# Final normalisation of a one-layer decoder: the weight vector multiplied in before the root is known, the row scale split between VectorE and ScalarE

## The chip, the cores and the metric

One core of one Trainium2 chip runs the whole program. The metric is the device time of one execution in microseconds (us). Differences of under 0.5% are taken as no difference that a measurement of this kernel can tell.

## The reference

One inference step of a hybrid decoder layer for 1024 prompt tokens and 32 sample tokens, D = 1024. The first two thirds (projection, RWKV-7 mixing, windowed attention, output projection, routing) are not touched. What matters here is the end:

```python
x = x + hier_moe(rmsnorm(x, norm_ffn_g))      # 16 experts, 2 per token, SwiGLU
y = rmsnorm(x, norm_final_g)                  # x * rsqrt(mean(x*x) + 1e-6) * norm_final_g
```

Every token needs, for its output row, the sum of squares of the finished row, the root of it, and a product with a scale per row and with the weight vector `norm_final_g` (`gfin`, spread over all 128 partitions).

## The kernel before

The experts are worked off one after the other, e = 0 to 15 (`NE` = 16), in an order sorted at run time. For each expert TensorE does four quarters f = 0 to 3 of gate and up (`gate_up`, L1544, 32 matmuls of 128x128 each), and then `down` (L1567, two halves of eight 128x512 matmuls). In TensorE's program order `down` of expert e - 1 stands after the first quarter of expert e, so the end of the program reads: quarter 0 of expert 15, down of 14, quarters 1, 2, 3 of expert 15, down of 15. For each quarter ScalarE takes the silu (L2087) and VectorE multiplies with the up half (`product`, L2792). Two banks of PSUM alternate between the quarters: quarter f of an expert is not started before the product of quarter f - 2 has read its bank, and down of an expert waits for all four products of it.

For experts 0 to 12 the weighted outputs are scattered into `x_dram`, the residual rows in HBM. The last three (13, 14, 15, `LAST` = 3) are dealt with apart: their rows are gathered out of `x_dram` into `xsA[0]` to `xsA[2]`, `sums` (L2891) adds the outputs of the expert on VectorE, and the sums are normalised by themselves and scattered straight to the outputs by GpSimd (`put`, L3052, two for each of the three experts).

All rows of `x_dram` are loaded when the scatters of expert 12 have landed: nine tiles `final_rows(t)`, t = 0 to 8, tiles 0 to 7 in the region `XF` (which held expert weights before), tile 8 (32 sample tokens) in a slot of `X2`. Those rows that the last three experts still touch are normalised and stored too, and are overwritten afterwards by `put`.

The final normalisation lies in the time of the last two experts:

- **Expert 14, ScalarE** (`before_last`): a square with a sum over the row for `xsA[0]` (f = 0) and for tiles 0 to 8 (f = 1 to 3, three each, L2103); after the last, one root over the ten sums (L2106, with a load of the table of the square root), and a dummy silu that loads the silu table again (L2110).
- **Expert 15, VectorE**: after product 0 it takes the reciprocal of the ten roots (L2948), `own` writes the normalised rows of expert 13 (L2899), `sums(1, 0)` and `sums(1, 1)` for expert 14, and `bulk(t)` for the nine tiles, each one instruction that does row scale and weight vector at once (L2896). Six `bulk` stand before product 1, three between product 1 and product 2.
- **Expert 15, ScalarE** (`at_last`): f = 0: a square of `xsA[1]`, which waits for `sums(1, 1)`; f = 2: its root, and the silu table again; f = 3: the table of the root. The silu of quarter f stands ahead of step f.
- **SP** stores the tiles in the order 0 to 8 (L742), each when its `bulk` is done (semaphore `fin`); the stores count on `h2o0` and `h2o1`.
- **GpSimd** waits for all nine stores, then for `fn_dve` of each group, and issues the six `put`.
- **The end**: `sums(2, h)` for the two halves of down of expert 15, squares, root, reciprocal and a last scaling by row (L2971) into `XF[:, 0, :]`, then the last two `put`. VectorE and ScalarE wait for the stores (`h2o0`, `h2o1`) before that, since `XF[:, 0, :]` is also tile 0.

Of the kernel before, what the change touches and what calls it, by code (L numbers as in the profile page):

```python
# [30 lines left out]
NE = NG * EPG  # L31
# [109 lines left out]
def program(nc, i, o):  # L141

    ctx = ExitStack()
    with ctx:
# [261 lines left out]
        YST = [stored(ACC, k) for k in range(2)]  # L406
        NDOWN = downs(NE)
        NOUT = NE + NTAIL
        FA, FD = 16, 4
        H2O = [32 * 4 + 16, 32 * 5 + 16]  # L410

        ps = ctx.enter_context(nc.psum_tensor("ps", [P, 8, 512], F32))
# [99 lines left out]
        def _(sp):  # L512
# [199 lines left out]
            def one_round(r, later):  # L712
                if later:
                    sp.wait_ge(s["ya_ps"], NDOWN * r)
                    alone(sp)
                    sp.wait_ge(s["fn_dve"], FD * r)
                    alone(sp)
                    for e in range(2):
                        x = expert(e)
                        load_pair(x, GU[e])  # L720
                        load_part(x, e, 2)
                    load_pair(expert(2), GU[2])
                for e in range(NE - 2):
                    sp.wait_ge(s["gu_ps"], 4 * (NE * r + e + 1))
                    alone(sp)
                    if GU[e] in GU[e + 1:]:
                        load_pair(expert(e + 1 + GU[e + 1:].index(GU[e])), GU[e])
                    else:
                        for k in range(2):
                            sp.wait_ge(s[f"yst{k}"], YST[k] * (r + 1))  # L730
                            alone(sp)
                        for n, (a, b) in enumerate(XL):
                            sp.dma_start(XF[:, a:b, :], x_rows[:, a:b]).then_inc(s[f"x{n}"], 16)
                        sp.dma_start(final_rows(NT), x_dram[SEQ:TOK]).then_inc(s["x3"], 16)
                    sp.wait_ge(s["ya_ps"], NDOWN * r + downs(e + 1))
                    alone(sp)
                    load_part(expert(e + 2), e % 2, 2)

                for t in range(NTT):
                    sp.wait_ge(s["fin"], NTT * r + t + 1)  # L740
                    dst = y_rows[t * P:(t + 1) * P, :] if t < NT else ys_rows
                    sp.dma_start(dst, final_rows(t)).then_inc(s[f"h2o{t % 2}"], 16)  # L742
                sp.wait_ge(s["h2o0"], H2O[0] + 16 * 5 * (r + 1))
                alone(sp)
                sp.wait_ge(s["h2o1"], H2O[1] + 16 * 4 * (r + 1))
                alone(sp)
# [894 lines left out]
        def _(act):  # L1641
# [455 lines left out]
            def one_round(r, later):  # L2097
# [23 lines left out]
                def before_last(f):  # L2121
# [7 lines left out]
                    if f == 3:  # L2129
                        act.wait_ge(s["fn_act"], fa + 10)  # L2130
                        root(10, stat[:, 0:10]).then_inc(s["fn_act"], 1)
                        table(ACT.Silu, 52)

                def at_last(f):
                    if f == 0:
                        act.wait_ge(s["yo_dve"], out0 + ACC + 1 + tails_to(ACC + 1) + 1)
                        act.wait_ge(s["fn_dve"], FD * r + 1)
                        square(eyA[:, 0, :], xsA[1], 32).then_inc(s["fn_act"], 1)
                    elif f == 2:
                        act.wait_ge(s["fn_act"], fa + 12)  # L2140
                        root(33, stat[:, 32:33]).then_inc(s["fn_act"], 1)
                        table(ACT.Silu, 53)
                    elif f == 3:
                        table(ACT.Sqrt, 54)
# [14 lines left out]
                        elif e == NE - 1:  # L2159
                            at_last(f)  # L2160

                act.wait_ge(s["h2o0"], H2O[0] + 16 * 5 * (r + 1))
                act.wait_ge(s["yo_act"], g0 + NE)
                square(X2[:, 2, 0:512], xsA[2][:, 0:512], 42).then_inc(s["fn_act"], 1)
                act.wait_ge(s["yo_dve"], out0 + NOUT)
                square(X2[:, 2, 512:], xsA[2][:, 512:], 43).then_inc(s["fn_act"], 1)
                act.wait_ge(s["fn_act"], fa + 15)
                act.wait_ge(s["fn_dve"], FD * r + 3)
                root(45, stat[:, 43:44], 0).then_inc(s["fn_act"], 1)

# [9 lines left out]
        def _(dve):  # L2180
# [623 lines left out]
            def one_round(r, later):  # L2804
# [85 lines left out]
                    x = xsA[k][:, 512 * h:512 * (h + 1)]  # L2890
                    dve.scalar_tensor_tensor(x, ps[:, 5 + h, :], wA[:, e:e + 1], x, ALU.mult, ALU.add).then_inc(s["yo_dve" if h else "yo_act"], 1)  # L2891

                def bulk(t):
                    n = toks(t)
                    x = final_rows(t)
                    dve.scalar_tensor_tensor(x, x, stat[0:n, 20 + t:21 + t], gfin[0:n, :], ALU.mult, ALU.mult).then_inc(s["fin"], 1)  # L2896

                def own(dst, k, rstd):
                    dve.scalar_tensor_tensor(dst, xsA[k], stat[:, rstd:rstd + 1], gfin, ALU.mult, ALU.mult).then_inc(s["fn_dve"], 1)  # L2899

                def after_last(f):
                    if f < 2:
                        for t in range(3):
                            bulk(3 * f + 3 + t)
                    elif f == 2:
                        dve.wait_ge(s["fn_act"], fa + 13)
                        again(dve.reciprocal(stat[:, 34:35], stat[:, 33:34]))
                        own(eyA[:, 0, :], 1, 34)

                slot_marks()  # L2910
                if later:
# [21 lines left out]
                for e in range(1, NE - 1):  # L2933
                    product(g0 + e, e, 0)
                    if 1 < e <= ACC:
                        rows_out(r, e - 1)
                    elif e > ACC:
                        for h in range(2):
                            sums(e - 1 - ACC, h)
                    product(g0 + e, e, 1)  # L2940
                    turn(r, e + 1)
                    for f in range(2, 4):
                        product(g0 + e, e, f)

                product(g0 + NE - 1, NE - 1, 0)
                dve.wait_ge(s["shift_in"], 64)
                dve.wait_ge(s["fn_act"], fa + 11)
                again(dve.reciprocal(stat[:, 20:30], stat[:, 10:20]))  # L2948
                own(eyA[:, 1, :], 0, 29)
                sums(1, 0)  # L2950
                bulk(0)
                sums(1, 1)
                bulk(1)
                bulk(2)
                after_last(0)
                for f in range(1, 4):
                    product(g0 + NE - 1, NE - 1, f)
                    after_last(f)
                sums(2, 0)
                dve.wait_ge(s["fn_act"], fa + 14)  # L2960
                dve.tensor_scalar(stat[:, 44:45], stat[:, 42:43], 1.0 / D, RMS_EPS, ALU.mult, ALU.add).then_inc(s["fn_dve"], 1)
                dve.wait_ge(s["h2o0"], H2O[0] + 16 * 5 * (r + 1))
                dve.wait_ge(s["h2o1"], H2O[1] + 16 * 4 * (r + 1))
                dve.wait_ge(s["yo_act"], g0 + NE)
                dve.tensor_tensor(XF[:, 0, 0:512], xsA[2][:, 0:512], gfin[:, 0:512], ALU.mult)
                sums(2, 1)
                dve.wait_ge(s["yo_dve"], NOUT * (r + 1))
                again(dve.tensor_tensor(XF[:, 0, 512:], xsA[2][:, 512:], gfin[:, 512:], ALU.mult))
                dve.wait_ge(s["fn_act"], fa + 16)
                again(dve.reciprocal(stat[:, 46:47], stat[:, 45:46]))  # L2970
                dve.tensor_scalar(XF[:, 0, :], XF[:, 0, :], stat[:, 46:47], None, ALU.mult).then_inc(s["fn_dve"], 1)  # L2971
                assert steps[0] == STEPS

            one_round(0, False)
# [8 lines left out]
        def _(pool):  # L2983
# [136 lines left out]
            pool.wait_ge(s["h2o0"], H2O[0] + 16 * 5 + 16 * 5 * past)  # L3120
            alone(pool)
            pool.wait_ge(s["h2o1"], H2O[1] + 16 * 4 + 16 * 4 * past)
            for k, out in enumerate((eyA[:, 1, :], eyA[:, 0, :], XF[:, 0, :])):
                e = ACC + k
                alone(pool)
                pool.wait_ge(s["fn_dve"], FD * past + (1, 2, 4)[k])
# [28 lines left out]
```

## Time and profile before

| | us |
|---|---|
| three runs | 1167.63, 1170.05, 1172.68 (median 1170.05) |
| the profiled execution | 1167.85 |
| span of it, first to last instruction | 1166.0 |
| time around the span | 1.85 |

Times in the profile count from the start of the span. An engine name with q (SPq, POOLq) is the sequencer or DMA queue of that engine; PEld is TensorE's weight load. In a timeline row the first figure is the start, the second the duration, and the bracket holds the idle time of the engine just before it and what ended it.

### The profile page before, as it was taken

The numbers are of one execution on the slowest core, as the hardware profiler recorded it, in microseconds if no ns is written. First come the engines' busy times: TensorE is split into PE (matmuls) and PEld (weight loads), VectorE is DVE, ScalarE is ACT, GpSimd is POOL, SyncE is SP. The second block draws the span as 40 slices with busy tenths as digits, with TensorE's granted clock in tenths as the row PEclk, the third lists the DMA queues.
The fourth block names the chain that finished last, engine by engine and source line by source line (L and its number), as shares of the span: only waits on it lengthen the run. The fifth ranks groups of instructions, "written<-read, shape, count | busy, mean of one in ns | idle before, by whom it ended". The sixth has DMA issues, their size and how long they took to land.

```text
span 1166.0 us, 23360 instructions
## 1 busy us (share of the span) xinstructions
PE 1099.5 (94%) x10010; PEld 773.1 (66%) x10010; DVE 499.0 (43%) x993; ACT 358.8 (31%) x816; POOL 299.7 (26%) x197
## 2 busy tenths in 40 slices
PE   5999999999999988888899999899999999999994
PEld 4666666666666667767654444587877887888782
DVE  3300566538865586686734422453111211221144
ACT  3110545554434375755621311210000000000052
POOL 0000000001110169999900000015313232233102
PEclk9999999999999999999999999889999999999997
DMA  6611100001110220002051751239999899999874
GB/s 206 162 36 39 59 19 19 19 19 41 33 30 19 26 48 3 4 4 57 4 203 26 266 209 67 95 140 397 380 389 320 315 320 330 336 314 303 279 268 168
DMA packets 69523, 174.06 MB, mean 149 GB/s; under 512 B 20708, under 2 KB 41895, under 8 KB 65172
## 3 DMA queue, kind: packets, MB, share of 16 engines
q1 hardware_dynamic: 61492, 151.92, 36.6%
q0 software_dynamic: 7920, 20.57, 7.1%
q8 instruction: 81, 1.33, 0.5%
q14 instruction: 30, 0.25, 0.1%
HBM read 147.45 MB, written 27.75 MB: 150 GB/s over the span
## 4 chain that ended last, share of the span: by engine, by line
PE 86%; DVE 9%; issue 2%; ACT 1%; SPq 0%; DMA 0%; POOLq 0%; POOL 0%; DVEq 0%
PE ps L810 23%; PE ps L1544 21%; PE ps L1328 10%; PE ps L1567 9%; PE ps L1573 1%; PE ps L889 1%; PE ps L913 1%; PE ps L902 1%; PE ps L1080 1%; DVE arena L2383 1%; PE ps L1202 1%; PE ps L1039 1%; PE ps L1408 1%; PE ps L1216 1%; PE ps L1138 1%
## 5 line engine op out<-in xcount | busy, mean ns | idle before, releaser
L810 PE MATMUL ps<-arena 128*128 128x352 f32 (+1 forms) x960 | 296.4, 465 | 2.1 <-issue 1.9
L1544 PEld LDWEIGHTS ps<-arena 128*128 128x128 f32 x2048 | 247.8, 192 | 10.5 <-issue 6.6
L1544 PE MATMUL ps<-arena 128*128 128x128 f32 (+4 forms) x2048 | 250.8, 284 | 3.3 <-DVE arena L2792 2.4
L810 PEld LDWEIGHTS ps<-arena 128*128 128x128 f32 x960 | 179.6, 190 | 105.1 <-issue 9.5
L1328 PE MATMUL ps<-arena 128*128 128x512 f32 x256 | 116.4, 597 | 0.7 <-DVE arena L2468 0.7
L1567 PE MATMUL ps<-arena 128*128 128x512 f32 x256 | 112.7, 593 | 1.4 <-DVE arena L2792 1.4
L2087 ACT ACTIVATE arena<-ps 128x128 f32<-128x128 f32 (+4 forms) x64 | 18.3, 285 | 270.3 <-PE ps L1544 270.3
L2990 POOL TENSOR_TENSOR arena<-arena 128x1024 f32<-128x1024 f32 x4 | 11.4, 2858 | 320.2 <-DVE arena L2269 320.2
L2792 DVE TENSOR_TENSOR arena<-arena,ps 128x128 f32<-128x128 f32 (+4 forms) x64 | 19.1, 299 | 172.6 <-ACT arena L2087 172.6
L1567 PEld LDWEIGHTS ps<-arena 128*128 128x128 f32 x256 | 47.5, 190 | 55.4 <-issue 53.6
L1328 PEld LDWEIGHTS ps<-arena 128*128 128x128 f32 x256 | 46.8, 190 | 52.8 <-issue 51.0
L3055 POOL DMA_INDIRECT arena<-h_dram,idxG x60 | 57.9, 964 | 82.8 <-DVE arena L2773 44.9
L3048 POOL DMA_INDIRECT x_dram<-arena,rowA x13 | 21.1, 1622 | 140.8 <-DVE arena L2802 102.1
L1658 ACT COPY arena<-ps 128x353 f32<-128x353 f32 (+1 forms) x40 | 18.0, 451 | 113.2 <-PE ps L810 113.2
L2799 DVE TENSOR_SCALAR arena<-ps,arena 128x512 f32<-128x512 f32 x13 | 9.8, 751 | 77.9 <-PE ps L1567 77.9
L3009 POOL TENSOR_TENSOR arena<-arena 128x1024 f32<-128x1024 f32 (+4 forms) x40 | 41.0, 1026 | 2.8
L2773 DVE STREAM_TRANSPOSE arena<-arena 128x256 f32<-128x256 f32 x68 | 37.4, 607 | 2.5 <-DMA arena<-h_dram,idxG 2.5
L1875 ACT COPY arena<-ps 64x256 f32<-64x256 f32 x80 | 29.4, 367 | 24.4 <-DVE ps L2405 23.1
L2314 DVE SCALAR_TENSOR_TENSOR arena<-ps,arena 128x1024 f32<-128x1024 f32 (+1 forms) x16 | 18.5, 1158 | 41.7 <-PE ps L889 41.7
L2581 DVE TENSOR_TENSOR arena<-arena,ps 128x512 f32<-128x512 f32 x16 | 11.0, 687 | 58.5 <-PE ps L1328 58.2
L1069 PE MATMUL ps<-arena 64*64 64x64 f32 x1280 | 29.6, 226 | 6.7 <-DVE arena L2389 5.8
L1728 ACT ACTIVATE arena<-arena 128x256 f32<-128x256 f32 (+1 forms) x64 | 30.9, 486 | 12.5 <-DVE arena L2320 12.5
(440 smaller groups left out, 1524.3 us busy)
## 6 DMA issues: line engine op xcount, KB each, us to landing
arena<-in_w_exp_gate SPq DMA_DIRECT2D x16, 2048.0 KB, 10.0
arena<-in_w_exp_up SPq DMA_DIRECT2D x16, 2048.0 KB, 14.5
arena<-in_w_exp_down SPq DMA_DIRECT2D x16, 2048.0 KB, 14.0
arena<-in_w_in SPq DMA_DIRECT2D x16, 512.0 KB, 3.8
arena<-in_x_prompt SPq DMA_DIRECT2D x9, 512.0 KB, 4.4
x_dram<-arena SPq DMA_DIRECT2D x9, 512.0 KB, 3.6
h_dram<-arena SPq DMA_DIRECT2D x8, 512.0 KB, 2.6
out_y_prompt<-arena SPq DMA_DIRECT2D x8, 512.0 KB, 3.5
```

The costliest lines, as they stand in the source:

```text
L810: last = pe.matmul(ps[:, q % 2, 0:m], wr[:, n % 3, k, :], hT[:, k, a:a + m], start=(k == 0), stop=(k == KB - 1))
L1069: last = pe.matmul(ps[row(e ^ u), 4 * b + u, j * CH:(j + 1) * CH], L[row(e), b, u, e, j, 0:CH], TL[row(e), b, JB * u + j, :], start=True, ...
L1328: return pe.matmul(ps[0:n, 4 * (q % 2) + hf, :], MX[:, b, t * P:t * P + n], wo[b][:, hf * 512:(hf + 1) * 512], start=(b == 0), stop=(b == 7))
L1544: last = pe.matmul(ps[:, 3 + f % 2, n * CAP:n * CAP + CAPS[e]], w[GU[e]][:, k, f * P:(f + 1) * P], xgT[:, a, k, 0:CAPS[e]], start=(k == 0) ...
L1567: last = pe.matmul(ps[:, 5 + n, :], eact[:, a, k, 0:P], edown[a][:, k, n * 512:(n + 1) * 512], start=(k == 0), stop=(k == 3))
L1728: last = act.activation(sc[:, u % 2, g, a:], sc[:, u % 2, g, a:], ACT.Exp, bias=ast[:, 4 * (u % 2) + g:4 * (u % 2) + g + 1], accum_out=ast ...
L1875: last = act.copy(TT[row(e), b, JB:2 * JB, :].rearrange("p j t -> p (j t)"), ps[row(1 - e), 4 * b + 2, 0:JB * CH])
L2773: return dve.transpose(xgT[:, a, :, b * XB:(b + 1) * XB], src.rearrange(LANES, k=KB))
L2792: dve.tensor_tensor(eact[:, a, f, 0:c], egl[:, f % 2, 0:c], ps[:, 3 + f % 2, CAP:CAP + c], ALU.mult).then_inc(s["ac_ok"], 1)
L3009: link(pool.tensor_tensor(stm[:, :, 0:m], stm[:, :, 0:m], stm[:, :, m:2 * m], ALU.add))
L3048: pool.indirect_dma_start(dst, bass.IndirectOffsetOnAxis(rows[:, e:e + 1], 0), src[:, e % 2, :], None, compute_op=ALU.add).then_inc(s[f"ys ...
L3055: return pool.indirect_dma_start(dst, None, src, bass.IndirectOffsetOnAxis(idx, 0))
```

## The change

`bulk` is split in two. `weighted(t)` multiplies tile t by the weight vector on VectorE as soon as ScalarE has squared it, before any root is known; these nine instructions move from expert 15 to the time of expert 14 (tiles 0 to 7) and to just after product 0 of expert 15 (tile 8). `scaled(t)` multiplies by the scale of the row: tiles 0 to 4 on VectorE (`BY_DVE` = 5), tiles 5 to 8 on ScalarE, where tiles 5 and 6 stand after silu 0 of expert 15 and wait for the reciprocal (`dve_r`), and tiles 7 and 8 after silu 1. Before product 1 VectorE now has three `scaled`, between product 1 and product 2 two. The square of `xsA[1]` stands behind `scaled(5)` and `scaled(6)` on ScalarE. The `own` of expert 14 stays between products 2 and 3. SP stores in the order 0, 5, 1, 6, 2, 3, 7, 4, 8. The rows of expert 15 get `X2[:, 0, :]` in the place of `XF[:, 0, :]`, and the waits of VectorE and ScalarE for the stores go.

```diff
@@ -406,7 +406,8 @@
         YST = [stored(ACC, k) for k in range(2)]
         NDOWN = downs(NE)
         NOUT = NE + NTAIL
-        FA, FD = 16, 4
+        FA, FD = 20, 4
+        BY_DVE = 5
         H2O = [32 * 4 + 16, 32 * 5 + 16]
 
         ps = ctx.enter_context(nc.psum_tensor("ps", [P, 8, 512], F32))
@@ -736,8 +737,11 @@
                     alone(sp)
                     load_part(expert(e + 2), e % 2, 2)
 
-                for t in range(NTT):
-                    sp.wait_ge(s["fin"], NTT * r + t + 1)
+                for t in (0, 5, 1, 6, 2, 3, 7, 4, 8):
+                    if t < BY_DVE:
+                        sp.wait_ge(s["fin"], BY_DVE * r + t + 1)
+                    else:
+                        sp.wait_ge(s["fn_act"], FA * r + (12, 13, 15, 16)[t - BY_DVE])
                     dst = y_rows[t * P:(t + 1) * P, :] if t < NT else ys_rows
                     sp.dma_start(dst, final_rows(t)).then_inc(s[f"h2o{t % 2}"], 16)
                 sp.wait_ge(s["h2o0"], H2O[0] + 16 * 5 * (r + 1))
@@ -2131,13 +2135,23 @@
                         root(10, stat[:, 0:10]).then_inc(s["fn_act"], 1)
                         table(ACT.Silu, 52)
 
+                def scaled(t):
+                    x = final_rows(t)
+                    act.activation(x, x, ACT.Copy, scale=stat[0:toks(t), 20 + t:21 + t]).then_inc(s["fn_act"], 1)
+
                 def at_last(f):
                     if f == 0:
+                        act.wait_ge(s["dve_r"], STEPS * (r + 1) - 3)
+                        scaled(5)
+                        scaled(6)
                         act.wait_ge(s["yo_dve"], out0 + ACC + 1 + tails_to(ACC + 1) + 1)
                         act.wait_ge(s["fn_dve"], FD * r + 1)
                         square(eyA[:, 0, :], xsA[1], 32).then_inc(s["fn_act"], 1)
+                    elif f == 1:
+                        scaled(7)
+                        scaled(8)
                     elif f == 2:
-                        act.wait_ge(s["fn_act"], fa + 12)
+                        act.wait_ge(s["fn_act"], fa + 16)
                         root(33, stat[:, 32:33]).then_inc(s["fn_act"], 1)
                         table(ACT.Silu, 53)
                     elif f == 3:
@@ -2159,12 +2173,11 @@
                         elif e == NE - 1:
                             at_last(f)
 
-                act.wait_ge(s["h2o0"], H2O[0] + 16 * 5 * (r + 1))
                 act.wait_ge(s["yo_act"], g0 + NE)
                 square(X2[:, 2, 0:512], xsA[2][:, 0:512], 42).then_inc(s["fn_act"], 1)
                 act.wait_ge(s["yo_dve"], out0 + NOUT)
                 square(X2[:, 2, 512:], xsA[2][:, 512:], 43).then_inc(s["fn_act"], 1)
-                act.wait_ge(s["fn_act"], fa + 15)
+                act.wait_ge(s["fn_act"], fa + 19)
                 act.wait_ge(s["fn_dve"], FD * r + 3)
                 root(45, stat[:, 43:44], 0).then_inc(s["fn_act"], 1)
 
@@ -2890,22 +2903,17 @@
                     x = xsA[k][:, 512 * h:512 * (h + 1)]
                     dve.scalar_tensor_tensor(x, ps[:, 5 + h, :], wA[:, e:e + 1], x, ALU.mult, ALU.add).then_inc(s["yo_dve" if h else "yo_act"], 1)
 
-                def bulk(t):
-                    n = toks(t)
+                def weighted(t):
                     x = final_rows(t)
-                    dve.scalar_tensor_tensor(x, x, stat[0:n, 20 + t:21 + t], gfin[0:n, :], ALU.mult, ALU.mult).then_inc(s["fin"], 1)
+                    dve.wait_ge(s["fn_act"], fa + 2 + t)
+                    dve.tensor_tensor(x, x, gfin[0:toks(t), :], ALU.mult)
+
+                def scaled(t):
+                    x = final_rows(t)
+                    dve.tensor_scalar(x, x, stat[0:toks(t), 20 + t:21 + t], None, ALU.mult).then_inc(s["fin"], 1)
 
                 def own(dst, k, rstd):
                     dve.scalar_tensor_tensor(dst, xsA[k], stat[:, rstd:rstd + 1], gfin, ALU.mult, ALU.mult).then_inc(s["fn_dve"], 1)
-
-                def after_last(f):
-                    if f < 2:
-                        for t in range(3):
-                            bulk(3 * f + 3 + t)
-                    elif f == 2:
-                        dve.wait_ge(s["fn_act"], fa + 13)
-                        again(dve.reciprocal(stat[:, 34:35], stat[:, 33:34]))
-                        own(eyA[:, 0, :], 1, 34)
 
                 slot_marks()
                 if later:
@@ -2939,36 +2947,47 @@
                             sums(e - 1 - ACC, h)
                     product(g0 + e, e, 1)
                     turn(r, e + 1)
-                    for f in range(2, 4):
-                        product(g0 + e, e, f)
-
+                    if e < NE - 2:
+                        product(g0 + e, e, 2)
+                        product(g0 + e, e, 3)
+
+                dve.wait_ge(s["shift_in"], 64)
+                weighted(0)
+                product(g0 + NE - 2, NE - 2, 2)
+                weighted(1)
+                weighted(2)
+                product(g0 + NE - 2, NE - 2, 3)
+                for t in range(3, 8):
+                    weighted(t)
                 product(g0 + NE - 1, NE - 1, 0)
-                dve.wait_ge(s["shift_in"], 64)
+                weighted(8)
                 dve.wait_ge(s["fn_act"], fa + 11)
                 again(dve.reciprocal(stat[:, 20:30], stat[:, 10:20]))
                 own(eyA[:, 1, :], 0, 29)
                 sums(1, 0)
-                bulk(0)
+                scaled(0)
                 sums(1, 1)
-                bulk(1)
-                bulk(2)
-                after_last(0)
-                for f in range(1, 4):
-                    product(g0 + NE - 1, NE - 1, f)
-                    after_last(f)
+                scaled(1)
+                scaled(2)
+                product(g0 + NE - 1, NE - 1, 1)
+                scaled(3)
+                scaled(4)
+                product(g0 + NE - 1, NE - 1, 2)
+                dve.wait_ge(s["fn_act"], fa + 17)
+                again(dve.reciprocal(stat[:, 34:35], stat[:, 33:34]))
+                own(eyA[:, 0, :], 1, 34)
+                product(g0 + NE - 1, NE - 1, 3)
                 sums(2, 0)
-                dve.wait_ge(s["fn_act"], fa + 14)
+                dve.wait_ge(s["fn_act"], fa + 18)
                 dve.tensor_scalar(stat[:, 44:45], stat[:, 42:43], 1.0 / D, RMS_EPS, ALU.mult, ALU.add).then_inc(s["fn_dve"], 1)
-                dve.wait_ge(s["h2o0"], H2O[0] + 16 * 5 * (r + 1))
-                dve.wait_ge(s["h2o1"], H2O[1] + 16 * 4 * (r + 1))
                 dve.wait_ge(s["yo_act"], g0 + NE)
-                dve.tensor_tensor(XF[:, 0, 0:512], xsA[2][:, 0:512], gfin[:, 0:512], ALU.mult)
+                dve.tensor_tensor(X2[:, 0, 0:512], xsA[2][:, 0:512], gfin[:, 0:512], ALU.mult)
                 sums(2, 1)
                 dve.wait_ge(s["yo_dve"], NOUT * (r + 1))
-                again(dve.tensor_tensor(XF[:, 0, 512:], xsA[2][:, 512:], gfin[:, 512:], ALU.mult))
-                dve.wait_ge(s["fn_act"], fa + 16)
+                again(dve.tensor_tensor(X2[:, 0, 512:], xsA[2][:, 512:], gfin[:, 512:], ALU.mult))
+                dve.wait_ge(s["fn_act"], fa + 20)
                 again(dve.reciprocal(stat[:, 46:47], stat[:, 45:46]))
-                dve.tensor_scalar(XF[:, 0, :], XF[:, 0, :], stat[:, 46:47], None, ALU.mult).then_inc(s["fn_dve"], 1)
+                dve.tensor_scalar(X2[:, 0, :], X2[:, 0, :], stat[:, 46:47], None, ALU.mult).then_inc(s["fn_dve"], 1)
                 assert steps[0] == STEPS
 
             one_round(0, False)
@@ -3120,7 +3139,7 @@
             pool.wait_ge(s["h2o0"], H2O[0] + 16 * 5 + 16 * 5 * past)
             alone(pool)
             pool.wait_ge(s["h2o1"], H2O[1] + 16 * 4 + 16 * 4 * past)
-            for k, out in enumerate((eyA[:, 1, :], eyA[:, 0, :], XF[:, 0, :])):
+            for k, out in enumerate((eyA[:, 1, :], eyA[:, 0, :], X2[:, 0, :])):
                 e = ACC + k
                 alone(pool)
                 pool.wait_ge(s["fn_dve"], FD * past + (1, 2, 4)[k])
```

## Rows read from the trace of the kernel before

**Rows 1.** The page: shares of the chain that ended last, by engine.
```profile
PE 86%; DVE 9%; issue 2%; ACT 1%; SPq 0%; DMA 0%; POOLq 0%; POOL 0%; DVEq 0%
```

**Rows 2.** The chain that ended last, in order of time: start us, duration us, what.
```profile
1133.75 5.98 DVE arena L2896 x5
...
1139.98 5.39 PE ps L1544 x32
...
1146.04 7.15 PE ps L1567 x16
```

**Rows 3.** Timeline, TensorE's quarters of gate and up, 128 and 64 matmuls.
```profile
1109.14 14.46 PE L1544 MATMUL ps<-arena 128*128 128x128 f32 x128
...
1130.30 7.31 PE L1544 MATMUL ps<-arena 128*128 128x128 f32 x64
```

**Rows 4.** Windows of 2 us: busy by engine, granted clock, DMA share, GB/s.
```profile
1138.00:1140.00 2.00, 0.02 (x1) 0.03 (x1) 2.00 (x4) 1.97 (x3) 0.00 (x0) 0.96 1.00 401
1140.00:1142.00 2.00, 2.00 (x9) 2.00 (x10) 2.00 (x2) 1.03 (x2) 0.00 (x0) 0.50 1.03 412
```

**Rows 5.** Timeline, VectorE and ScalarE, experts 14 (end) and 15.
```profile
1125.02 1.06 ACT L2103 ACTIVATE arena<-arena 32x1024 f32<-32x1024 f32 x1
...
1129.49 0.29 DVE L2792 TENSOR_TENSOR arena<-arena,ps 128x128 f32<-128x128 f32 x1 [6.45 <-ACT arena L2087]
1129.70 0.21 DVE L2948 RECIPROCAL stat<-stat 128x10 f32<-128x10 f32 x1
...
1133.78 1.06 ACT L2103 ACTIVATE arena<-arena 128x1024 f32<-128x1024 f32 x1 [4.32 <-DVE arena L2891]
...
1134.84 0.26 ACT L2087 ACTIVATE arena<-ps 128x128 f32<-128x128 f32 x1
1137.64 0.28 ACT L2087 ACTIVATE arena<-ps 128x128 f32<-128x128 f32 x1 [2.55 <-PE ps L1544]
...
1139.64 0.28 DVE L2792 TENSOR_TENSOR arena<-arena,ps 128x128 f32<-128x128 f32 x1
...
1140.84 0.20 ACT L2110 ACTIVATE stat<-eps 128x1 f32<-128x1 f32 x1
...
1145.39 0.28 ACT L2087 ACTIVATE arena<-ps 128x128 f32<-128x128 f32 x1 [4.35 <-PE ps L1544]
```

**Rows 6.** Groups by line and form, whole span: count, busy us, mean ns, idle before.
```profile
L2274 DVE TENSOR_TENSOR arena<-arena 128x1024 f32<-128x1024 f32 x4 | 10.6, 2659 | 0.0
...
L2211 DVE TENSOR_SCALAR arena<-arena,stat 128x1024 f32<-128x1024 f32 x8 | 6.0, 753 | 0.3
...
L2273 DVE TENSOR_TENSOR arena<-arena 128x1024 f32<-128x1024 f32 x4 | 4.9, 1218 | 0.0
...
L2094 ACT ACTIVATE arena<-ps,arena 128x512 f32<-128x512 f32 x13 | 8.9, 687 | 42.6 <-PE ps L1567 42.6
...
L2087 ACT ACT_TABLE_LOAD x1 | 1.3, 1283 | 0.0
...
L2062 ACT ACTIVATE arena<-arena,stat 128x1024 f32<-128x1024 f32 x1 | 1.1, 1150 | 0.0
```

**Rows 7.** Timeline, stores (SPq), scatters of the last groups (POOL), last DVE steps.
```profile
1133.11 9.56 SPq L742 DMA_DIRECT2D out_y_prompt<-arena  x8
...
1143.52 0.33 SPq L742 DMA_DIRECT2D out_y_sample<-arena  x1
...
1147.42 1.01 POOL L3052 DMA_INDIRECT out_y_prompt<-arena,rowA  x1 [22.03 <-issue]
...
1151.34 0.98 POOL L3052 DMA_INDIRECT out_y_sample<-arena,smpA  x1 [0.30 <-issue]
...
1151.56 0.69 DVE L2965 TENSOR_TENSOR arena<-arena 128x512 f32<-128x512 f32 x1
...
1157.05 0.98 POOL L3052 DMA_INDIRECT out_y_prompt<-arena,rowA  x1 [4.74 <-DVE arena L2971]
```

**Rows 8.** DMA issues of the end: count, KB each, us from issue to landing.
```profile
out_y_sample<-arena SPq DMA_DIRECT2D x1, 128.0 KB, 2.6
```

## The prediction

> **What bounds the kernel now.** I read the page first. TensorE holds 86% of the chain that ended last and VectorE 9% [rows 1], so an edit outside TensorE is worth only what it takes out of TensorE's waits, or out of the tail behind its last matmul. The chain in order of time shows where VectorE enters it within the stage that the change touches: five `bulk` of 5.98 us together stand on the chain, then the last quarter of gate and up (x32), then, after a silu and a product, down of expert 15 [rows 2]. So TensorE waits for VectorE there. The timeline of TensorE gives the size. Quarters 1 and 2 of expert 15 start at 1130.30 and take 7.31, so they end at 1137.61; the third starts at 1139.98: TensorE stands still for 2.37 us [rows 2, 3].
>
> The reader should then look at the third quarter itself. Four quarters took 14.46, so one takes 3.62; this one took 5.39, which is 1.77 more [rows 2, 3]. The windows say why: the granted clock was 0.96 in the stretch in which TensorE was idle and 0.50, the lower of its two levels (1.2 GHz), in the stretch after it [rows 4]. So the late product costs 2.37 + 1.77 = 4.14 us, not 2.37. The timeline of VectorE shows that product 1 began at 1139.64 though its silu was there at 1134.84 + 0.26 = 1135.10 [rows 5]: it stood behind six `bulk` on its own engine. VectorE was, on the other hand, idle for 6.45 us ahead of product 0 at 1129.49, from 1123.04 on [rows 5]. That hole is where the change puts its products with the weight vector.
>
> Last, the two things that could take over. The puts of the last two groups wait for the stores of all nine tiles: the last store is issued at 1143.52 and lands 2.6 later, at 1146.1, and the first put starts at 1147.42 [rows 7, 8]. Four puts come before the last group's; from the first to the fourth there are 1151.34 - 1147.42 = 3.92 us, so 1.31 a step, and the fifth could start at 1147.42 + 4 x 1.31 = 1152.65. It starts at 1157.05 [rows 7]: the put queue has 4.4 us to spare, and more than that can't be won here.
>
> **The change, part by part.**
>
> *The nine `weighted`.* Each is a 128x1024 product of two tiles on VectorE; the same form took 1218 ns at L2273 and up to a mean of 2659 at L2274 [rows 6]. I take 1.22, since at L2274 GpSimd ran arithmetic at the same time, while in the end stage it only issues indirect DMAs, and a VectorE product that starts inside such a DMA (1151.56, in the put of 1151.34) took an ordinary 0.69 for half the width [rows 7]. Tiles 0 to 2 go in front of and between the products of expert 14, where one costs a fraction of a quarter's 3.62. Tiles 3 to 7 start at 1123.04 and end by 1123.04 + 5 x 1.22 = 1129.14, still ahead of product 0 at 1129.49, and the last square they follow is done before 1125.02 [rows 5]. So eight of nine cost nothing; the idle 6.45 us cover them, and without that cover they would cost 6.1. Tile 8 stands behind product 0 and costs 1.22.
>
> *VectorE from product 0 to `sums(1, 1)`.* Before: reciprocal, `own`, sums, `bulk(0)`, sums. After: `weighted(8)` ahead of it (+1.22), `scaled(0)` for `bulk(0)`: a scaling by row took 753 ns at L2211 against 5.98/5 = 1.20 of a `bulk` (-0.45) [rows 2, 6]. Sum +0.77. ScalarE's square of `xsA[1]` follows `sums(1, 1)` and moves from 1133.78 to 1134.55, silu 1 from 1134.84 to 1135.61, and product 1 with it to about 1135.9, ending at 1136.2 [rows 5]. The new `scaled(5)` and `scaled(6)` on ScalarE wait for the reciprocal, 1129.70 + 1.22 + 0.21 = 1131.13, and take 1.15 each by the one row of exactly this form, L2062 [rows 5, 6]: done at 1133.4, before the square could start. Queued behind that wait are the square and silu 1, and neither is ready before it ends. A Copy with a row scale needs no table load: L2094 did 13 of them between silus, and L2087 shows one load in the whole span [rows 6].
>
> *TensorE's third quarter.* Product 1 at 1136.2 is 1.4 us before quarter 2 ends at 1137.61, so the wait of 2.37 goes, and with it, I take it, the lower clock: the quarter runs from 1137.61 to 1141.23 in place of 1145.37.
>
> *What is late next.* ScalarE. `scaled(7)` and `scaled(8)` follow silu 1 and end at 1135.9 + 2 x 1.15 = 1138.2, so silu 2 starts at 1138.2 and not at 1137.64. From silu 2 to the end of the dummy silu (root of expert 14 with two table loads) it took 1140.84 + 0.20 - 1137.64 = 3.40 [rows 5]; silu 3 starts at 1141.6, 0.4 after its quarter has ended. Before, that block was hidden behind the late quarter (silu 3 at 1145.39). VectorE has the reciprocal and `own` of expert 14 in front of product 3, done about when silu 3 is. So down of expert 15 starts 1145.39 - 1141.6 = 3.8 us earlier, at 1142.25 [rows 2, 5].
>
> Of ScalarE's price for a row scaling the Trainium skill says, in "Trainium Architecture — The Big Picture", The five engines, in one table, that simple arithmetic isn't for ScalarE, VectorE being up to about three times as fast per element; by an estimate from that, a tile would take 3 x 0.753 = 2.26 and the gain shrink to some 0.5 us. The trace says 1.15.
>
> *Stores.* The first can start 0.77 later than 1133.11, like `sums(1, 1)`; the transfers already ran at 401 to 412 GB/s with a DMA share of 1.00 and more [rows 4, 7], so more rows ready at once don't make them faster. From first issue to last landing it took 13.0 us; the 4.33 MB (8 x 512 KB + 128 KB) alone need 10.7 at 405 GB/s. So the landing lies between 1.5 earlier and 0.8 later; I take the later, 1146.9. The fifth put could then start at 1152.65 + 0.8 = 1153.45; VectorE's end, moved by 3.8, allows 1157.05 - 3.8 = 1153.25. The two are nearly level, and the later one leaves 3.6 for the gain.
>
> *The region of their own.* It removes waits for stores that land at 1146.1; VectorE's write stood at 1151.56 [rows 7], so it waited for nothing, and now stands at 1147.8, still later than 1146.9. Worth nothing by itself; without it, a landing 1 us later would hold up the end.
>
> **Sum.** The profiled execution: 1167.85 - 3.6 = 1164.25. That execution lies 2.2 below the median of the runs; against the median it is 1170.05 - 3.6 = 1166.4. The runs themselves spread over 5 us; 0.5%, about what a measurement of this kernel can tell from no change, is 5.9 us, more than this gain.
>
> **Rivals.**
>
> *The stores set the end.* Four more rows come ready close together and are stored in a fixed order; if the last lands 2 us later than 1146.9, the fifth put starts 2 us later still, and each further microsecond costs one. Gain 1.6, time 1168.4. For it: the two ends were level. Against it: a full DMA share already before.
>
> *The clock falls all the same.* Then quarter 3 takes 5.39 and ends at 1143.0; the gain is the 2.37 of the wait alone, time 1167.7. Against it: quarters 1 and 2 ran at full speed after down of 14 without a pause.
>
> *ScalarE becomes the bound.* At a price of a for a tile, silu 1 moves to 1131.13 + 2a + 1.06 once that exceeds 1135.61, and silu 3 to 0.26 + 2a + 3.40 after it; it is back at 1145.39 for a = 2.4, and the gain is gone: time 1170. Against it: L2062 with 1.15, and the square with 1.06 [rows 5, 6]. The Trainium skill's sentence above is this rival's rule.
>
> *Slower: the moved products don't fit the hole.* If GpSimd's gather or ScalarE's squares slow them to p each, product 0 starts at 1123.04 + 5p, and product 1 ends 6.7 - 1.22 + p after it. TensorE starts the third quarter no earlier than before once 1123.04 + 5p + 5.5 + p reaches 1139.95, so from p = 1.90 on. At the 2.66 of L2274 it starts at 1144.5, 4.5 later: 1174.6 [rows 5, 6]. Against it: the undisturbed 0.69 [rows 7].
>
> **How the numbers follow.** Forecast 0.78, stores 0.08, clock 0.06, ScalarE 0.04, slower 0.04. The forecast's own range is 1162.5 to 1169, most of it from the spread of the runs. The three rivals that shrink the gain lie at 1167.7 to 1170, so the range is 1162 to 1170, and it leaves out the slower one and the edges of the spread. Faster by over 0.5% means below 1164.2; the forecast's spread of about 2.5 us puts a quarter of its 0.78 there: 0.19. Slower by over 0.5% is above 1175.9, 0.02. The rest, 0.79, is within.
>
> **What would show it.** In the changed trace: product 1 starts near 1136 relative to product 0 at 1129.5; no idle time of TensorE between quarters 2 and 3; quarter 3 near 3.6 us at a granted clock of 1.0; silu 3 waits for ScalarE's own queue and not for TensorE; the fifth put follows the fourth within half a microsecond. I am wrong if product 0 starts after 1129.6, if quarter 3 still shows a clock of 0.50, or if the first put starts after 1149.

## The result, and the profile after

The changed kernel took 1226.53 us (median of four runs, 1226.25 to 1228.76), the kernel before 1168.84 beside it: ratio 1.0495, 95% interval 1.0474 to 1.0516. It is 5% slower, where the prediction had 1166.4 and a range up to 1170.

The surprise is that the stage which the change touches did what was forecast. Timeline of the changed kernel, same stretch as [rows 3, 5, 7]:

```profile
1122.05 5.76 DVE L2909 TENSOR_TENSOR arena<-arena 128x1024 f32<-128x1024 f32 x5
...
1123.15 7.03 PE L1571 MATMUL ps<-arena 128*128 128x512 f32 x16
...
1128.58 0.29 DVE L2805 TENSOR_TENSOR arena<-arena,ps 128x128 f32<-128x128 f32 x1 [0.77 <-ACT arena L2091]
...
1130.02 10.88 PE L1548 MATMUL ps<-arena 128*128 128x128 f32 x96
1130.15 2.19 ACT L2140 ACTIVATE arena<-arena,stat 128x1024 f32<-128x1024 f32 x2 [1.60 <-DVE stat L2965]
...
1134.80 0.29 DVE L2805 TENSOR_TENSOR arena<-arena,ps 128x128 f32<-128x128 f32 x1
...
1137.36 0.28 ACT L2091 ACTIVATE arena<-ps 128x128 f32<-128x128 f32 x1 [0.52 <-PE ps L1548]
...
1140.94 0.28 ACT L2091 ACTIVATE arena<-ps 128x128 f32<-128x128 f32 x1 [0.17 <-PE ps L1548]
...
1141.59 7.13 PE L1571 MATMUL ps<-arena 128*128 128x512 f32 x16 [0.69 <-DVE arena L2805]
...
1147.01 1.01 POOL L3071 DMA_INDIRECT out_y_prompt<-arena,rowA  x1 [21.79 <-issue]
...
1152.59 0.97 POOL L3071 DMA_INDIRECT out_y_prompt<-arena,rowA  x1 [0.69 <-issue]
1153.87 0.98 POOL L3071 DMA_INDIRECT out_y_sample<-arena,smpA  x1 [0.30 <-issue]
```

Five `weighted` fit ahead of product 0; product 1 comes at 1134.80, well before TensorE needs it; quarters 1 to 3 of expert 15 are one run of 96 matmuls in 10.88 us without a pause, 3.63 each. Down of 15 starts 18.44 us after down of 14 (1123.15, 1141.59), where it was 22.61 before (1123.43, 1146.04). The last put, the sixth, is issued at 1153.87; before it was at 1158.33. The two rows of the kernel before:

```profile
1123.43 7.03 PE L1567 MATMUL ps<-arena 128*128 128x512 f32 x16
...
1158.33 0.98 POOL L3052 DMA_INDIRECT out_y_sample<-arena,smpA  x1 [0.30 <-issue]
```

And yet the span is 1224.9. What lies between? The windows behind the last put:

```profile
1160.00:1180.00 20.00, 0.00 (x0) 0.00 (x0) 0.00 (x0) 0.00 (x0) 0.00 (x0) 0.50 0.02 4
1180.00:1200.00 20.00, 0.00 (x0) 0.00 (x0) 0.00 (x0) 0.00 (x0) 0.00 (x0) 0.50 0.02 4
1200.00:1220.00 20.00, 0.00 (x0) 0.00 (x0) 0.00 (x0) 0.00 (x0) 0.00 (x0) 0.50 0.02 5
```

No engine computes anything, and some 4 GB/s are moved. The DMA queues of the stretch 1160 to 1220 say what they are:

```profile
q14 instruction: 32, 0.26, 2.0%
```

They are instructions: 32 packets in 60 us, of 0.26 MB / 32 = 8 KB each. Over the whole span the page has 66 on that queue, and the kernel before 30; first the line of after, then that of before:

```profile
q14 instruction: 66, 0.53, 0.2%
```

```profile
q14 instruction: 30, 0.25, 0.1%
```

Which engine fetches? The list of waits on SP's queue answers wrongly at first sight; its longest wait in the changed kernel is

```profile
SPq L144 <- PEq L144: 67.7, 1, 67.7
```

L144 is where the program ends, a barrier of all engines, and the releaser is inferred. The instructions on L144 themselves, that is the sequencers' last drains ahead of the barrier (duration in ns, first and last start), show who came last:

```profile
L144 POOLq DRAIN  x1: 8126/8126/8126, 1152.9 to 1152.9; - x1
L144 PEldq DRAIN  x1: 8/8/8, 1153.1 to 1153.1; - x1
...
L144 ACTq DRAIN  x1: 8/8/8, 1158.6 to 1158.6; - x1
L144 DVEq DRAIN  x1: 46/46/46, 1224.7 to 1224.7; - x1
```

It is VectorE, at 1224.7; GpSimd was done at 1161.0. What VectorE did until then stands on the two lines of its loop over later rounds, `with dve.Fori(1, ROUNDS) as r` and `with dve.If(rounds > r)`. There are 9 - 1 = 8 passes, and with one round needed none enters the body. The sequencer's rows, changed kernel (L2996 the loop, L2997 the test):

```profile
L2996 DVEq MOVE  x9: 36/36/57, 1152.5 to 1218.7; - x9
L2996 DVEq ALU_OP  x8: 40/40/52, 1155.5 to 1222.2; - x8
L2996 DVEq COMPARE_BRANCH  x8: 50/56/56, 1157.9 to 1224.6; - x8
...
L2997 DVEq COMPARE_BRANCH  x8: 69/69/73, 1152.6 to 1218.8; - x8
```

and the same loop in the kernel before (L2977):

```profile
L2977 DVEq MOVE  x9: 36/36/57, 1156.3 to 1164.5; - x9
L2977 DVEq ALU_OP  x8: 40/40/52, 1159.5 to 1164.9; - x8
L2977 DVEq COMPARE_BRANCH  x8: 50/56/72, 1159.6 to 1164.9; - x8
```

Eight ALU_OPs (the loop's counter) lie between 1155.5 and 1222.2, so a pass takes 66.7/7 = 9.5 us; before it was 5.4/7 = 0.77. The instructions themselves are as short as before, under 0.1 us. The last row of each is to be read against the row above it: after the last counter step at 1222.2 the branch behind it, the very next instruction, starts at 1224.6, 2.4 us later. Before, both read 1164.9. The jump from the test (1218.8) to the counter (1222.2) takes 3.4 us, and at 9.5 us a pass the 32 packets in 60 us are five a pass.

In the kernel before the loop was hidden. Its last drains (same view):

```profile
L144 POOLq DRAIN  x1: 8440/8440/8440, 1157.4 to 1157.4; - x1
...
L144 DVEq DRAIN  x1: 17/17/17, 1165.0 to 1165.0; - x1
```

GpSimd's drain ended at 1157.4 + 8.4 = 1165.8, after VectorE had come.

### The profile page after: what moved, and what is told of

It reads as the page before. It is cut to its first block, busy times and chain, and to the rows that moved or that the text cites. A ratio compares the mean times of both kernels' runs of the same rounds, so it can differ in the third digit from the quotient of the medians.

```text
span 1224.9 us, 23367 instructions
## 1 busy us (share of the span) xinstructions
PE 1097.8 (90%) x10010; PEld 771.1 (63%) x10010; DVE 501.9 (41%) x998; ACT 362.7 (30%) x820; POOL 300.2 (25%) x197
## 4 chain that ended last, share of the span: by engine, by line
PE 82%; DVE 8%; issue 2%; ACT 1%; DMA 1%; SPq 0%; POOL 0%; POOLq 0%; DVEq 0%
PE ps L814 22%; PE ps L1548 20%; PE ps L1332 9%; PE ps L1571 8%; PE ps L1577 1%; PE ps L893 1%; PE ps L917 1%; PE ps L906 1%; PE ps L1084 1%; DVE arena L2396 1%; PE ps L1142 1%; PE ps L1043 1%; PE ps L1183 1%; PE ps L1412 1%; PE ps L1206 1%
## 5 line engine op out<-in xcount | busy, mean ns | idle before, releaser
L2786 DVE STREAM_TRANSPOSE arena<-arena 128x256 f32<-128x256 f32 x68 | 37.4, 608 | 2.5 <-DMA arena<-h_dram,idxG 2.5
L2327 DVE SCALAR_TENSOR_TENSOR arena<-ps,arena 128x1024 f32<-128x1024 f32 (+1 forms) x16 | 18.5, 1158 | 43.3 <-PE ps L893 43.3
```

The source lines that it names most:

```text
L2786: return dve.transpose(xgT[:, a, :, b * XB:(b + 1) * XB], src.rearrange(LANES, k=KB))
```

## The experiments

Two spans tell the runs apart, both from the start of down of expert 14: to the sixth put (the stage), and to the end. The whole time is less sharp for this: down of 14 starts between 1120.9 and 1128.1 in runs whose program up to there is the same within a few empty instructions.

| run | us | down of 14 to sixth put | to the end of the span | passes on VectorE |
|---|---|---|---|---|
| before | 1167.85 | 34.90 | 42.6 | 8 x 0.77 |
| changed | 1226.76 | 30.72 | 101.8 | 8 x 9.5 |
| shift1 | 1165.31 | 31.00 | 38.6 | short |
| shift64 | 1170.72 | 31.02 | 38.7 | short |
| shift160 | 1170.52 | 31.00 | 38.6 | short |
| before_shift18 | 1233.64 | 33.54 | 103.9 | long |
| body1 | 1168.30 | 30.73 | 38.4 | short |
| body128 | 1224.35 | 31.11 | 101.0 | long |
| head12 | 1167.80 | 31.00 | 39.2 | short |
| head11 | 1225.35 | 30.72 | 99.3 | long |
| guard_border | 1160.78 | 30.72 | 38.1 | none |
| guard | 1163.68 | 30.72 | 38.1 | none |
| region_back | 1165.06 | 31.07 | 38.7 | short |
| all_dve | 1164.47 | 31.00 | 38.6 | short |

The table has the profiled execution of each. Before, changed, shift160, body1 and guard were timed several times; the others ran once, so there the two spans and the rows of the loop carry the argument, and not a few microseconds of the total.

Three theories were put to the test. The first, border: the loop's end lies on a border between two pieces of the instruction stream, a pass needs three pieces (the head's, and one on either side of the border), and they push one another out. The second, window: the loop must lie within one stretch of fixed length. The third, length: the body has simply grown too long. The change puts the end of VectorE's loop 18 instructions further on, 4 of them in the first round and 14 in the body, by a count of the program.

**One empty instruction** at the start of VectorE's program (`alone` counts a semaphore that nobody waits for):

```diff
 def _(dve):
+    for _n in range(1):      # 64, 160, 12, 11, and 18 in the kernel before
+        alone(dve)
     chain = [0]
```

> The changed kernel with one empty instruction (it only counts a semaphore up) at the start of VectorE's program, so that everything VectorE does lies one instruction further on in its stream. In the changed trace VectorE walks through eight passes of the loop over later rounds, none of them taken, at about 9.5 us a pass, where it took 0.76 before; a long pause stands between the two last instructions of the loop. Theory 1, border: those two instructions lie on either side of a border between two pieces of the stream as it is fetched, a pass needs three pieces and fetches them anew each time; one instruction further on both lie behind the border, so the passes are short and the time is some 62 us less, about 1164. Theory 2, window: what counts is whether all the code from the head of the loop to its end lies within the stretch that is held; then one instruction more changes nothing, about 1226. Theory 3, length: the body grew too long for what is held, wherever it lies; about 1226.

1165.31, 61 us less, with the stage as it was but for 0.3 us (31.00 against 30.72):

```profile
L2998 DVEq MOVE  x9: 36/36/57, 1153.6 to 1161.8; - x9
L2998 DVEq ALU_OP  x8: 40/40/52, 1156.9 to 1162.2; - x8
L2998 DVEq COMPARE_BRANCH  x8: 50/56/72, 1156.9 to 1162.3; - x8
```

Nothing but the place of the code was changed. Theories two and three fall in the form in which they were put.

> As the run with one empty instruction, with 64 of them. Theory 1, border: both ends of the loop well inside a piece, about 1164. Theory 2, window: with pieces of 128 instructions and four held in a row the loop fits again, about 1164; with two pieces of 256 in a row it doesn't, 1210 to 1226. Theory 3, length: about 1226.

1170.72, with short passes, and the same 38.7 us at the end; the rest lies ahead of the stage, where down of 14 started at 1130.17; why so late is not shown. Border holds, and the window of two pieces of 256 is out.

> As the run with one empty instruction, with 160 of them. Theory 1, border, and theory 2, window, in either size: the loop is cheap again, about 1164, and the stage before it as in the changed kernel, so that against the kernel before about 4.5 us are left as gain (ratio 0.996). Theory 3, length: about 1226.

The loop is cheap again, but the time isn't lower: 1171.86 (ten runs) against 1169.0, ratio 1.0028, interval 1.0008 to 1.0049. This part of the expectation missed. The 160 empty instructions stand in front of VectorE's first work, which starts at 16.1 us where it started at 0.9 in shift1: TensorE is busy for 30.5 us of the first 50, against 37.4 in the changed kernel, and what is lost there (6.9) is more than the stage gains.

> The kernel before with 18 empty instructions at the start of VectorE's program; the end of its loop then lies where that of the changed kernel lies, and nothing else of the change is in it. Theory 1, border: about 60 us more than before, some 1230. Theory 2, window with four pieces of 128: no change, 1168; with two pieces of 256: some 1230. Theory 3, length: no change, 1168.

1233.64: the kernel before, with nothing of the change in it, becomes slow in the same way. Its loop:

```profile
L2979 DVEq MOVE  x9: 36/36/57, 1159.8 to 1225.7; - x9
L2979 DVEq ALU_OP  x8: 40/40/52, 1163.3 to 1229.1; - x8
L2979 DVEq COMPARE_BRANCH  x8: 50/56/56, 1165.9 to 1231.4; - x8
```

The gap from the last counter step to the branch behind it is there again (1229.1, 1231.4). So the slowness has nothing to do with what the change computes. A window of four pieces of 128 in a row, by which nothing would have changed here, is out too.

**Empty instructions in the body that is never entered.** These cost no time to execute.

```diff
+if later:
+    for _n in range(1):      # or 128
+        alone(dve)
 slot_marks()
 if later:
     capped_slots()
```

> The changed kernel with one empty instruction inside the loop body of VectorE that is never entered: nothing more is executed, the head of the loop stays where it is, its end lies one instruction further on, behind the border. Theory 1, border: the cost of the eight passes goes, and what is left is the gain of the last stage, 4 us, so about 1165 against 1169 (ratio 0.9965). Theory 3, length: the body is longer still, so 1226.

1167.31 (median of 12) against 1169.22: ratio 0.9971, interval 0.9951 to 0.9991. The body is longer than in the changed kernel and the loop is cheap: length is out. What is left to the change is 0.3%, and that is under the 0.5% that counts as a difference here.

> The same with 128 empty instructions in the body that is never entered. Theory 1, border, with pieces of 128 instructions: the last two instructions of the loop lie on either side of the next border, 9.5 us a pass, about 1226. With pieces of 256 they don't, and the time is about 1165.

1224.35, and the gap at the loop's end is back:

```profile
L2999 DVEq MOVE  x9: 36/36/57, 1150.2 to 1216.2; - x9
L2999 DVEq ALU_OP  x8: 40/40/52, 1153.6 to 1219.7; - x8
L2999 DVEq COMPARE_BRANCH  x8: 50/56/56, 1156.2 to 1222.2; - x8
```

So another border follows 128 instructions later, where pieces of 256 counted from the first border would have none.

> The changed kernel with 12 empty instructions at the start of VectorE's program, so that, with pieces of 128 instructions, the border lies between the two instructions at the head of the loop and no longer between those at its end. Theory 1, border: a pass again needs three pieces, about 1226, with the long pause now between the two instructions of the head. If the head doesn't count, or pieces are 256 long: about 1165.

1167.80, short passes: the border was not met, or the head doesn't count. The next run tells which.

> As the run with 12 empty instructions at the start, with 11: between the two instructions that the border may have to lie between at the head of the loop, if one branch of the written program has no instruction of its own. If the head on a border costs like the end on a border: about 1225, with 9 us a pass. If not: about 1166, and the head's place doesn't matter or was not met.

1225.35. Now the gap stands between the two instructions of the head, the MOVE of the loop (L2998) and the test behind it (L2999), and no longer at the end:

```profile
L2998 DVEq MOVE  x9: 36/36/57, 1153.5 to 1217.2; - x9
L2998 DVEq ALU_OP  x8: 40/40/52, 1157.7 to 1223.1; - x8
L2998 DVEq COMPARE_BRANCH  x8: 59/66/66, 1157.8 to 1223.2; - x8
...
L2999 DVEq COMPARE_BRANCH  x8: 69/69/73, 1154.0 to 1219.6; - x8
```

The last MOVE is at 1217.2 and the test at 1219.6, 2.4 us later, while counter and branch at the end are 0.1 apart (1223.1, 1223.2). A border at either place makes three pieces of two, and the price is the same. 12 instructions were one too many.

**No passes at all.**

```diff
-with dve.Fori(1, ROUNDS) as r:
-    with dve.If(rounds > r):
-        one_round(r, True)
+with dve.If(rounds > 1):
+    with dve.Fori(1, ROUNDS) as r:
+        with dve.If(rounds > r):
+            one_round(r, True)
```

> The loop over later rounds on VectorE is put under a test of its own that is made once (more than one round), and the end of the loop lies on a border of pieces of 128 instructions (127 empty instructions in the body that is never entered). The passes alone cost the time by every theory, and none is made: about 1164. If something else at the end of the changed kernel were late, it would stay at 1226.

1160.78, and 38.1 us from down of 14 to the end, with the loop's end, by the count, on a border of the 128 grid. The whole 60 us were passes. The low total is in part an early start (down of 14 at 1120.86).

> The changed kernel with the one test around VectorE's loop over later rounds, and no empty instructions: no pass is made, and the place of the loop in the stream no longer matters. From the start of down of expert 14 to the end 38.0 us, as in the run with the test and the loop's end on a border, against 42.55 before; so 4.5 us under the kernel before, ratio 0.996. If the passes were hidden behind the end of GpSimd anyway, it is no better than with one empty instruction in the body (38.3 us, ratio 0.997).

1165.47 (median of 12) against 1170.57: ratio 0.9974, interval 0.9954 to 0.9994. It takes the 5% back; against the kernel before it is 0.3% again, under the 0.5%, and within the intervals no better than one empty instruction in the body. From down of 14 to the end it is 0.3 us shorter than body1. More could not be won, since in body1 even the cheap passes were over (VectorE's drain at 1165.8) before GpSimd's drain was (1157.9 + 8.4 = 1166.3).

**Parts of the change, with the loop off the border.** First the region and the waits put back:

```diff
-dve.tensor_tensor(X2[:, 0, 0:512], xsA[2][:, 0:512], gfin[:, 0:512], ALU.mult)
+dve.wait_ge(s["h2o0"], H2O[0] + 16 * 5 * (r + 1))
+dve.wait_ge(s["h2o1"], H2O[1] + 16 * 4 * (r + 1))
...
+dve.tensor_tensor(XF[:, 0, 0:512], xsA[2][:, 0:512], gfin[:, 0:512], ALU.mult)
```

(and the other places of `X2[:, 0, ...]`, and ScalarE's wait for `h2o0`).

> The changed kernel with the rows of the last expert in the region of tile 0 again and the waits of VectorE and ScalarE for the stores (the two waits shift the end of VectorE's loop off the border). By the prediction the region is worth nothing: 38.3 to 39 us from the start of down of expert 14 to the end. If the stores land later than VectorE wants to write, the last put starts that much later: 39.5 us or more.

31.07 and 38.7, against 30.7 to 31.0 and 38.4 to 38.6: worth nothing, as forecast. Then all nine row scalings on VectorE:

```diff
+BY = (0, 1, 2, 5, 6, 3, 4, 7, 8)
...
-act.wait_ge(s["dve_r"], STEPS * (r + 1) - 3)
-scaled(5)
-scaled(6)
...
-scaled(7)          # on ScalarE
-scaled(8)
...
-scaled(1)          # on VectorE, ahead of product 1
-scaled(2)
+for t in BY[1:5]:
+    scaled(t)
 product(g0 + NE - 1, NE - 1, 1)
-scaled(3)
-scaled(4)
+for t in BY[5:]:
+    scaled(t)
```

(SP stores in the order `BY`, and the counts of the semaphores follow.)

> All nine tiles scaled by VectorE, four more of 0.67 us each: tiles 0, 1, 2, 5, 6 ahead of product 1, tiles 3, 4, 7, 8 between products 1 and 2; ScalarE has none (the loop's end lies off the border). If the gain of the stage comes from the product with the weight vector having been moved, product 1 still comes before TensorE needs it (it moves by 1.3 us, and there were 2.5), and down of 14 to down of 15 takes 18.4 us as in the changed kernel. If ScalarE's share is what frees VectorE, TensorE waits again before the third quarter: 20 us or more, towards the 22.6 of before.

```profile
1123.95 7.03 PE L1569 MATMUL ps<-arena 128*128 128x512 f32 x16
...
1130.82 10.88 PE L1546 MATMUL ps<-arena 128*128 128x128 f32 x96
...
1134.37 2.73 DVE L2905 TENSOR_SCALAR arena<-arena,stat 128x1024 f32<-128x1024 f32 x4
...
1137.02 0.28 DVE L2797 TENSOR_TENSOR arena<-arena,ps 128x128 f32<-128x128 f32 x1
...
1142.39 7.13 PE L1569 MATMUL ps<-arena 128*128 128x512 f32 x16 [0.69 <-DVE arena L2797]
```

Down of 14 to down of 15 is 1142.39 - 1123.95 = 18.44, the same to a hundredth. Product 1 is at 1137.02, before quarter 2 ends (1130.82 + 2/3 of 10.88 = 1138.07). ScalarE's share is worth nothing here; the gain is the moved product with the weight vector and the shorter row scaling.

## Why the prediction was wrong

The step that failed is the one from the last put to the end. Under **Sum**, the prediction took the gain of the fifth put, 3.6 us, off the whole time, as if what follows the put kept its length. What stood there was VectorE's loop over later rounds. In the kernel before it ended at 1164.9, 1.1 us ahead of the end, and was hidden by GpSimd's drain; the prediction read no row behind the fifth put at 1157.05, though 9.0 us of the span lie there, and named no cover for the loop, though the change lengthens VectorE's program in front of that loop and inside its body. The loop went from 1164.9 - 1156.3 = 8.6 us to 1224.6 - 1152.5 = 72.1, 63.5 more; it started 3.8 earlier, and of the 1.1 us behind it 0.3 are left: 63.5 - 3.8 - 0.8 = 58.9, which is 1224.9 - 1166.0. No rival had this mechanism; the slower one, products that don't fit the hole, did not happen. None of the three things by which the prediction would have known itself wrong came about either: all three lie within the stage.

Why a pass cost so much is read from the rows of the loop: 8 KB packets on an instruction queue, 2.4 us at the step that crosses a border and 3.4 at the jump behind the test. The Trainium skill has a rule for it, in "Runtime: NRT & Kernel Launch", Instruction fetch mechanics: each engine holds only a small stretch of its program, its sequencer fetches more by a DMA queue of its own, and a taken branch whose target isn't held must wait for the fetch. The trace agrees with that. The size that was measured differs: by the Trainium skill a block has 256 instructions and two are held, while here borders lie 128 instructions apart (body128, head11).

In the cheap passes two places of code far apart, the loop's head and its end, stay held: from 1158 us on shift1 has no packet on an instruction queue. Where a border runs through the head or through the end, a pass needs three pieces, and every pass fetches. It fetches five packets and not three; what the other two hold, how many pieces are held, and in what order they are given up is not shown.

The other steps, in order:

- *What bounds the kernel* was right: TensorE's wait of 2.37 is gone, and quarter 3 takes 3.63 in place of 5.39, at a granted clock of 1.00 in the windows from 1136 to 1142.
- *The nine `weighted`*: forecast 1.22 each and hidden but for one; measured 5.76 for five, 1.15 each, and product 0 waits for its silu and not for them.
- *Product 1* was forecast 6.4 us after product 0 started, and came after 6.2.
- *ScalarE late next* was mis-sized: two row scalings took 2.19 and not 2.30, silu 2 waited for TensorE, and silu 3 waited 0.17 for TensorE and not 0.4 for ScalarE. ScalarE's price of 1.1 us a tile settles its rival; on VectorE a tile took 0.75. The Trainium skill's "up to about 3× faster" between the two ("Trainium Architecture — The Big Picture", The five engines) is not reached in this form.
- *The stores* were forecast 0.8 later; the first put is 23.86 us after the start of down of 14, and was 23.99. They were not later in this execution. In seven of the twelve runs with the changed stage (shift1, shift64, shift160, body128, head12, region_back, all_dve) the first put came 24.2 to 24.6 us after down of 14; there the fifth put followed the fourth at once, at 1.36 to 1.41 us, so the put queue and not VectorE set its time. So the two ends were as level as the prediction had them, at a cost of 0.3 us; why the first put moves is open.
- *The fifth put* was forecast 3.6 to 3.8 earlier and at most half a microsecond behind the fourth; it waited 0.69. To the sixth put the stage is 34.90 - 30.72 = 4.2 us shorter; in shift1 3.9. With the loop off the border the whole is 0.3% faster by two timed kernels (0.9971, 0.9974), which is what 3.6 of 1170 would have been; by the 0.5% that is not yet a difference, and the gain is shown by the stage and not by the whole time.

## What to carry to other kernels

Before trusting a gain in the middle of a program, follow it to the end on every engine, sequencers included: list what each still has to do after its last computing instruction, and what hides it. A loop whose passes are skipped costs its branches, and an edit anywhere ahead of it or inside its body can move its head or its end onto a border of the instruction stream; put the whole loop under one test, or check the rows of its counter and branch after each edit. When a long stretch shows no busy engine, look at the instruction queue among the DMA queues and at each sequencer's last instruction, and don't take the releaser that the waits infer at a barrier for the culprit.

## What the runs showed that was not expected

A pass over code that is not entered costs 0.77 us or 9.5 us by nothing but its place in the program, and one empty instruction makes the difference; the border may lie at the head of the loop or at its end.

The lower clock after TensorE's wait is not a fixed price. In the kernel before, a wait of 2.37 was followed by a granted clock of 0.50 [rows 4], and quarter 3 took 5.39. In before_shift18, which has the same code in that stage, the wait was 1.72 (timeline):

```profile
1143.79 3.84 PE L1544 MATMUL ps<-arena 128*128 128x128 f32 x32 [1.72 <-DVE arena L2794]
1149.15 7.13 PE L1567 MATMUL ps<-arena 128*128 128x512 f32 x16 [1.52 <-DVE arena L2794]
```

and the clock stayed at full speed; windows:

```profile
1143.00:1145.00 2.00, 1.21 (x10) 1.21 (x11) 2.00 (x4) 1.97 (x3) 0.00 (x0) 1.00 1.03 410
1145.00:1147.00 2.00, 2.00 (x20) 2.00 (x19) 2.00 (x2) 0.50 (x2) 0.00 (x0) 1.00 1.02 406
```

Quarter 3 was 5.39 - 3.84 = 1.55 us shorter, but down of 15 then waited 1.52 for product 3 and not 0.69, which is 0.83 more; to the sixth put the stage took 33.54 us against 34.90. So in these two executions only about half of what the lower clock cost quarter 3 reached the put, where the prediction put all 1.77 into its price. What decides between the two levels is not shown.
